# Two transformer blocks on one core: depthwise conv and its projections placed in the linear attention, layer-norm statistics in the diff heads, full-height scores, mask by VectorE

## The chip, the cores and the metric

The kernel runs on one core of a Trainium2 chip. A core has a matrix engine (TensorE, PE in the profile), three engines for elementwise work (VectorE or DVE, ScalarE or ACT, GpSimd or POOL), and SyncE (SP), which here issues all DMAs. The metric is the device time of one execution in microseconds (us). Matrix products accumulate in PSUM, which TensorE, VectorE and ScalarE reach and GpSimd does not.

## The reference, cut to what matters

Sequence 1024, width 1024, float32. A first block (grouped attention, a linear recurrence, a gated network) isn't touched. The second block computes from `h = rms_norm(x)` one wide projection, and from its parts three branches:

```python
def conv_module(a, gate, w_dw, ln_g, ln_b, w_pw):      # 31-tap causal depthwise conv, 1024 channels
    u = a * jax.nn.sigmoid(gate)
    u = lax.conv_general_dilated(u, rhs, ..., padding=[(CONV_KERNEL - 1, 0)], feature_group_count=CONV_WIDTH)
    u = jax.nn.silu(layer_norm(u, ln_g, ln_b))
    return u @ w_pw
...
# gla: 4 heads of gated linear attention, key width 128, value width 256, in chunks of 64
...
# diff_attention: 8 heads, each with two score maps of key width 64 and a value width of 128
        s = jnp.einsum('bqhtd,bkhtd->bhtqk', qi, k) * scale
        mask = key_chunk[None, :] <= q_chunk[:, None]        # chunks of 64
        p = jax.nn.softmax(jnp.where(mask, s, -jnp.inf), axis=-1)
        pd = p[:, :, 0] - lam * p[:, :, 1]
        return jnp.einsum('bhqk,bkhv->bqhv', pd, v)
...
y = (jax.nn.sigmoid(m_conv) * o_conv + jax.nn.sigmoid(m_gla) * o_gla + jax.nn.sigmoid(m_diff) * o_diff)
x = x + y @ w_out[l]
```

Then come an RMS norm and a gated feed-forward network, which aren't touched either.

## The kernel before, in words

**Data.** Activations lie with 128 channels on the partitions and 1024 positions along each, as 8 tiles of 128 x 1024. Every large product is done in three passes: both operands are split into a high part (rounded to the format fp32r) and a low part (the rest), and hi x hi, hi x lo, lo x hi are added up.

**A job** (`job`, L480) is one output tile of 128 x 1024: 8 steps over k, each with 3 passes and 2 halves of 512 columns, so 48 matmuls. Its step over one k, 6 matmuls, is called a unit here. `job(..., ks=...)` does some of the 8 units. Jobs alternate between two PSUM slots and two weight slots; a third and a fourth PSUM slot serve the attention. The jobs have a fixed order, `J_GLA`, `J_DIFF` and so on, which the host lays the weights out by. For job j SyncE loads the raw weights (`load`, L768, waits until the low part of job j-2 is made), ScalarE makes the high part (`split_act`, L455, waits until job j-2 is done), GpSimd the low part (`splits_pool`, L472). Each engine runs its own instructions strictly in the order written; semaphores order them between engines.

**Linear attention** (`gla_head_act`, `gla_head_dve`, `gla_head_pe`): 4 heads in a loop on each engine, 8 jobs each (v twice, q, k, output gate twice, mixing gate twice). VectorE makes the decayed k and q, masks the scores and adds up the states.

**Diff heads** (`diff_head_act`, `diff_head_dve`, `diff_head_pe`, L2810): head 0, heads 1 to 6 in a loop, head 7. Before head 0 stand 6 jobs. In each of heads 0 to 6 stand 6 jobs for the next head: conv gate, conv value, mixing gate, v, q, k. In head 7 stand 4 of the 8 jobs of the conv branch's mixing gate, and 4 after it. In a head the queries go in 8 blocks of 128 (qt), with (qt+1) x 128 keys each, rounded up to 256. For each block and each of the two maps t:

- TensorE: `scores2` (qt under 4: both maps in one PSUM slot) or `scores(qt, t)` (qt 4 to 7: one map at a time; t = 1 waits for the exponential of t = 0, because both use the slot). The key width is 64, so a matmul fills half of the 128 rows. The three passes of one map go to the upper rows and the others to the lower rows; for qt over 3 swapped copies let the second half of the keys use the other rows (L2846, L2847). A matmul of bf16 rows of -1e30 adds the mask (L2824).
- VectorE: the negated row maximum (L2350). ScalarE: exponential with row sum (L1796).
- VectorE, after both (`combine`): reciprocals, product with lambda, scaling of map 0 (L2358), map 1 times its factor added (L2359).
- TensorE: `turn`, transposes of the result (L2853). ScalarE: `evac`, their copy (L1801). TensorE: `pv`, product with v (L2859).

Between these, `fill(u0, u1)` lets TensorE do units of the head's jobs: 3 between the two score maps, 4 before `turn`, 1 between `turn` and `pv`, of 48 in all; head 7 takes two thirds of each count. `pv` of block 7 and the norm of a head's output (square, sum over partitions by a matmul with ones, rsqrt by Ln and Exp on ScalarE and a Newton step on VectorE) stand in the next head.

**Conv.** `taps` (L2301) are the 31 multiply-adds over 128 x 1024 on VectorE, one channel tile per diff head: the first 16 in the head before, the other 15 in the head itself, in pieces between the other VectorE work. The finished tile is added to a running sum (L2378) and stored to DRAM by SyncE.

**Tail.** After head 7: sum of the running sum (mean), 8 tiles reloaded from DRAM and centred (L2582), squared (L2013), added up (L2597), a second sum, rsqrt, then per tile scale (L2601), Silu (L2027), high part (L2031) and low part (L1630), which the 8 jobs of the conv branch's last projection (`J_PW`) need. Then come the mix of the branches, the output projection (`J_OUT2`) and the feed-forward stage.

Of the kernel before, what the change touches and what calls it, by code (L numbers as in the profile page):

```python
# [52 lines left out]
J_DIFF = J_GLA + 32  # L53
J_MC = J_DIFF + 48
J_PW = J_MC + 8
# [123 lines left out]
def two_blocks(nc, x, w, cols, consts, rope, out):  # L179
    with ExitStack() as ctx:  # L180
# [171 lines left out]
        DKL = scratch("dk_lo", [P, S], F32R, 7)
# [5 lines left out]
        CG = scratch("cg_tanh", [P, S], F32, 14)  # L358
        DO, DSQ, DV, DY = (scratch(f"do_{c}", [P, S], F32, 15 + i) for i, c in enumerate(("out", "sq", "v", "y")))
        UC = scratch("u_pad", [P, S + 32], F32, 19)  # L360
        ACC = scratch("conv_again", [P, 8, S], F32, 0)
        MC = [scratch(f"mc_tanh{i}", [P, S], F32, t) for i, t in enumerate(MC_AT)]
        LA_, LV, LYY = (scratch(f"ln_{c}", [P, S], F32, t) for t, c in ((15, "a"), (17, "v"), (18, "y")))
        SSL = scratch("ln_sum_squares", [P, S], F32, 16)
        LT = scratch("ln_mean", [P, S], F32, 11)
        SQLN = [scratch(f"ln_sq{i}", [P, S], F32, 9 + i) for i in range(2)]
        CENTRE = (2, 3, 4, 5, 6, 7, 0, 1)
        gate_spill = nc.dram_tensor("gate_spill", (P, S), F32, kind="Internal").ap()
# [411 lines left out]
        def sync_program(sp):  # L780
# [2339 lines left out]
```

## Time and profile before

| | before |
|---|---|
| time of 3 runs, us | 3457.49, 3460.99, 3462.90 |
| median, us | 3460.99 |
| profiled execution: span, us | 3460.9 |
| TensorE busy | 3361.4 us, 97% |
| VectorE busy | 2208.2 us, 64% |
| ScalarE busy | 1435.1 us, 41% |
| GpSimd busy | 1121.9 us, 32% |
| granted TensorE clock, mean | 0.990 |
| DMA, mean | 70 GB/s |

The profiled execution's own time is known by its span, from the first to the last instruction. In the profile the linear attention lies at about 1285 to 1717 us, the first 6 diff jobs at 1718 to 1784, the diff heads at 1784 to 2535, the tail after them up to about 2620. Matmuls are pipelined: the time of a single one contains its way through the array, so the distance from start to start is what counts.

### The profile page before, as it was taken

To read this page: it belongs to the slowest core of one execution; us is meant where nothing else is said; L and a number is where in the kernel's file an instruction comes from. 1 tells how busy PE (TensorE), PEld (TensorE's weight loads), DVE (VectorE), ACT (ScalarE), POOL (GpSimd) and SP (SyncE) were. 2 spreads that over 40 slices of the span, in tenths; PEclk is the share of its full clock that TensorE was granted. 3 is DMA by queue.
4 is the path that set the end of the run, shared out by engine and by line. 5 is a ranking of instruction groups with operands and counts; after the bars stand their busy time and mean duration, and the time that the engine had idled before them with its cause. 6 is when DMAs were issued, how large, how long until landed. Compare 5 with 4: busy or idle time off the path is not lost.

```text
span 3460.9 us, 44771 instructions
## 1 busy us (share of the span) xinstructions
PE 3361.4 (97%) x16616; PEld 2710.6 (78%) x16616; DVE 2208.2 (64%) x2246; ACT 1435.1 (41%) x1901; POOL 1121.9 (32%) x644
## 2 busy tenths in 40 slices
PE   8899899999999999999999999999889999999998
PEld 6677777888888868888877777777668878888886
DVE  8896968777773474322277888888856574444434
ACT  5688835444441142333223443344453353333213
POOL 2000028888832212111111111111112276766222
PEclk9999999999999999999999999999999999999999
DMA  4210221222252112111111111111122212123322
GB/s 143 62 44 19 73 88 66 84 85 79 85 196 95 47 43 92 36 42 36 36 49 43 37 42 35 38 42 36 43 79 85 79 61 91 74 90 121 134 88 83
DMA packets 59167, 242.52 MB, mean 70 GB/s; under 512 B 6592, under 2 KB 6592, under 8 KB 53312
## 3 DMA queue, kind: packets, MB, share of 16 engines
q1 hardware_dynamic: 59072, 241.22, 19.7%
q8 instruction: 63, 1.03, 0.1%
q14 instruction: 32, 0.26, 0.0%
HBM read 194.53 MB, written 41.42 MB: 68 GB/s over the span
## 4 chain that ended last, share of the span: by engine, by line
PE 81%; DVE 12%; issue 3%; ACT 3%; DMA 0%; POOL 0%; DVEq 0%; POOLq 0%; ACTq 0%
PE ps L506 45%; PE ps L1457 24%; PE ps L2696 2%; PE ps L2708 2%; PE ps L2685 1%; PE ps L2846 1%; PE ps L2859 1%; DVE conv_acc L2310 1%; PE ps L529 1%; DVE t_wide L1094 1%; PE ps L2798 1%; PE ps L2853 1%; PE ps L2832 1%; DVE small L2350 1%; PE ps L2794 1%
## 5 line engine op out<-in xcount | busy, mean ns | idle before, releaser
L477 POOL TENSOR_TENSOR w_lo_part<-w_raw,w_hi_part 128x1024 fp32r<-128x1024 f32 x162 | 404.5, 2497 | 1739.0 <-ACT w_hi_part L460 1739.0
L506 PE MATMUL ps<-h_hi_part,w_hi_part 128*128 128x512 f32 x1904 | 625.4, 409 | 34.9 <-POOL w_lo_part L477 12.4
L506 PE MATMUL ps<-h_lo_part,w_hi_part 128*128 128x512 f32 x1904 | 596.5, 394 | 0.0
L506 PE MATMUL ps<-h_hi_part,w_lo_part 128*128 128x512 f32 x1904 | 594.9, 393 | 0.0
L460 ACT ACTIVATE w_hi_part<-w_raw 128x1024 fp32r<-128x1024 f32 x180 | 189.1, 1051 | 720.0 <-PE ps L506 632.4
L506 PEld LDWEIGHTS ps<-h_hi_part,w_hi_part 128*128 128x128 f32 x1904 | 348.1, 191 | 130.4 <-issue 37.2
L506 PEld LDWEIGHTS ps<-h_lo_part,w_hi_part 128*128 128x128 f32 x1904 | 361.7, 190 | 78.5 <-issue 0.3
L506 PEld LDWEIGHTS ps<-h_hi_part,w_lo_part 128*128 128x128 f32 x1904 | 361.4, 190 | 78.7
L2310 DVE SCALAR_TENSOR_TENSOR conv_acc<-u_pad,cols,conv_acc 128x1024 f32<-128x1024 f32 x232 | 307.4, 1325 | 19.4 <-DVE conv_acc L2310 2.8
L2149 DVE TENSOR_TENSOR residual<-residual,ps 128x1024 f32<-128x1024 f32 (+1 forms) x60 | 73.2, 1221 | 268.7 <-PE ps L506 262.2
L506 PE MATMUL ps<-u_hi,w_hi_part 128*128 128x512 f32 x736 | 232.0, 390 | 0.0
L506 PE MATMUL ps<-u_lo,w_hi_part 128*128 128x512 f32 x736 | 231.2, 389 | 0.0
L506 PE MATMUL ps<-u_hi,w_lo_part 128*128 128x512 f32 x736 | 231.1, 389 | 0.0
L1457 PE MATMUL ps<-t_hi,s_hi 128*128 128x512 f32 x552 | 216.2, 392 | 1.2 <-ACT copy_x L1161 0.7
L1457 PE MATMUL ps<-t_hi,s_lo 128*128 128x512 f32 x552 | 215.2, 390 | 0.0
L1457 PE MATMUL ps<-t_lo,s_hi 128*128 128x512 f32 x552 | 214.7, 389 | 0.0
L1796 ACT ACTIVATE dprob<-ps,small 128x256 f32<-128x256 f32 (+7 forms) x128 | 94.4, 740 | 241.3 <-DVE small L2350 241.0
L506 PEld LDWEIGHTS ps<-u_lo,w_hi_part 128*128 128x128 f32 x736 | 138.2, 188 | 29.2 <-issue 0.5
L506 PEld LDWEIGHTS ps<-u_hi,w_hi_part 128*128 128x128 f32 x736 | 138.2, 188 | 29.1 <-issue 0.5
L506 PEld LDWEIGHTS ps<-u_hi,w_lo_part 128*128 128x128 f32 x736 | 138.2, 188 | 28.7
L1457 PE MATMUL ps<-b_hi,a_hi 128*128 128x512 f32 x368 | 144.0, 391 | 0.0
L1457 PE MATMUL ps<-b_hi,a_lo 128*128 128x512 f32 x368 | 143.2, 389 | 0.0
(446 smaller groups left out, 6583.1 us busy)
## 6 DMA issues: line engine op xcount, KB each, us to landing
w_raw<-in_w SPq DMA_DIRECT2D x226, 512.0 KB, 3.3
w_raw_odd<-in_w SPq DMA_DIRECT2D x46, 512.0 KB, 3.9
u_spill<-ffn_u SPq DMA_DIRECT2D x46, 512.0 KB, 3.0
u_wide<-u_spill SPq DMA_DIRECT2D x23, 1024.0 KB, 9.2
residual<-in_x SPq DMA_DIRECT2D x4, 1024.0 KB, 9.0
both_halves<-q_chan SPq DMA_DIRECT2D x16, 256.0 KB, 4.3
x_again<-in_x SPq DMA_DIRECT2D x8, 512.0 KB, 3.9
residual<-in_x SPq DMA_DIRECT2D x2, 2048.0 KB, 7.2
```

The lines of the kernel that those rows point to most:

```text
L460: act.activation(WHI[:, slot, 0:nk], WRAW[:, slot, 0:nk], ACT.Copy).then_inc(w_hi, 1)
L477: pool.tensor_tensor(WLO[:, slot], WRAW[:, slot], f32(WHI[:, slot]), ALU.subtract).then_inc(w_ready, 1)
L506: last = pe.matmul(PS[:, ps, b * HALF:(b + 1) * HALF], st[:, slot, k, :], at(mv, k, b), start=(k == 0 and n == 0), stop=(k == nk - 1 and n ...
L529: mm = pe.matmul(PS[:, slot, b * HALF:(b + 1) * HALF], ones, src[:, b * HALF:(b + 1) * HALF], start=first, stop=last)
L1094: return dve.scalar_tensor_tensor(to, a, gain, b, ALU.mult, ALU.subtract)
L1457: last = pe.matmul(bank(to), st[op][:, k, :], of[mv][:, k, :], start=(first and k == 0 and n == 0), stop=(k == 3 and n == 2), skip_group_c ...
L1796: act.activation(DP[t][:, 0:n], PS[:, 2, at:at + n], ACT.Exp, bias=small(NEGM + 2 * qt + t), accum_out=small(RSUM + 2 * qt + t)).then_inc( ...
L2149: dve.tensor_tensor(dst, src, psl(slot, True), ALU.add).then_inc(ps_free[slot], 1)
L2310: st.do(dve.scalar_tensor_tensor(ACC1[:, :], UC[:, i:i + S], wgt, ACC1[:, :], ALU.mult, ALU.add))
L2350: dve.tensor_reduce(small(NEGM + 2 * qt + t), PS[:, 2, at:at + n], AX.X, ALU.max, negate=True).then_inc(dm_ready, 1)
L2696: mm = pe.transpose(PS[:, 0, k * P:k * P + P], PR[g % 2][:, k * P:k * P + P], con("ident"))
L2708: mm = pe.matmul(PS[64 * t:64 * t + 64, 1, qt * P:qt * P + P], VT[:, k, 64 * kv:64 * kv + 64], PT[2 * (q % 2) + t][:, k, :], start=(k == 0 ...
```

## The change

The number of jobs is the same; 16 of them (conv gate and value of 8 tiles) stand in the linear attention now, two pairs per head.

- *Order of jobs.* Linear attention: v, v, q, k, conv gate, conv value, output gates, mixing gates, conv gate, conv value (12 per head). Before diff head 0: v, q, k. In diff heads 0 to 4: conv mixing gate, v, mixing gate, q, k (5 jobs, 40 units). In heads 5 and 6 the same without the conv mixing gate (32 units). In head 7: three conv mixing gates and mixing gate 7 (32 units). The last projection goes in the order 5, 6, 0, 1, 2, 3, 4, 7.
- *Loops* over heads are unrolled on all engines but GpSimd.
- *Taps.* In head h of the linear attention VectorE does all taps of tile 2h and of tile 2h-1. Tile 7 follows before and in diff head 0. Tiles are stored to DRAM as before.
- *Scores.* The moving tiles K1 (k_hi twice, one copy on each half of the rows) and K2 (k_lo and zeros), and the stationary Q1 (q_hi and q_lo), are 128 rows high: two passes per map instead of three. The number of keys is rounded less (to 128, at least 256 columns a matmul).
- *Mask.* VectorE writes -1e30 into PSUM before it takes the maximum.
- *Fills.* 21 steps in proportion to `STEPS`; `combine` scales map 0 ahead, in `scale`.
- *Statistics.* Mean in head 1; tiles reloaded, centred, squared, added up and stored again in heads 2 to 5; the variance sum in head 6; rsqrt in head 6; scale and Silu of tiles 0 and 1 in head 7.
- *Conv mixing gates* of heads 0 to 4 are stored to DRAM and reloaded in the tail.
- The norm and the add of diff head 7 stand after the second tile of the last projection.

```diff
+HEAD_JOBS = [([("mc", h)] if h < 5 else []) + [("dv", h + 1), ("md", h), ("dq", h + 1), ("dk", h + 1)] for h in range(7)]
+HEAD_JOBS.append([("mc", 5), ("mc", 6), ("mc", 7), ("md", 7)])
+PW_ORDER = (5, 6, 0, 1, 2, 3, 4, 7)
...
         def gla_head_dve(dve, st, h):
+            if h:
+                taps(dve, st, 2 * h - 1, 0, 21)
             dve.wait_ge(g_exp, h * 4 + 4)
             dve.wait_ge(job_done, 2 * jp + 3)
             dve.scalar_tensor_tensor(GB[0][:, :], psl(0), P ** -0.5, GB[0][:, :], ALU.mult, ALU.mult).then_inc(ps_free[0], 1)
+            if h:
+                taps(dve, st, 2 * h - 1, 21, 28)
...
+            if h:
+                taps(dve, st, 2 * h - 1, 28, 31)
+                conv_sum(dve, st, 2 * h - 1)
...
             states(0)
             states(1)
+            conv_u_dve(dve, n)
             states(2)
             states(3)
+            taps(dve, st, n, 0, 6)
+            gate(0)
+            taps(dve, st, n, 6, 15)
...
+            taps(dve, st, n, 15, 19)
+            gate(1)
+            taps(dve, st, n, 19, 31)
+            conv_sum(dve, st, n)
...
             def row_max(qt, t):
                 dve.wait_ge(ds_done, h * 16 + (2 * qt + t + 1))
+                st.do(dve.memset(PS[0:CH, 2, at + n - CH:at + n], -1e30))
...
+            def scale(qt):
+                dve.wait_ge(e_done, ROUNDS + h * 16 + (2 * qt + 1))
+                st.do(dve.reciprocal(small(RINV + 2 * qt), small(RSUM + 2 * qt)))
+                st.do(dve.tensor_scalar(DP[0][:, 0:n], DP[0][:, 0:n], small(RINV + 2 * qt), None, ALU.mult))
...
         def diff_k_act(act, h):
+            for t in range(2):
+                act.activation(K1[t][OWN[t], :], out_of(("dk", h), OWN[t]), ACT.Copy).then_inc(dq_hi, 1)
+            act.wait_ge(dq_hi, h * 8 + 4)
+            diff_copies_act(act, K1, K1, OTHER, OWN, LEFT)
+            split_for(act, j + 2)
...
         def diff_head_act(act, st, h):
             evac(0)
+            diff_copies_act(act, K1, K1, OTHER, OWN, RIGHT)
...
             evac(1)
+            if h < 5:
+                m_conv_act(act, h, MCS)
             exp(2, 0)
             exp(2, 1)
             evac(2)
+            if 2 <= h <= 5:
+                centred_square_act(act, 2 * h - 4)
+            if h in (5, 6):
+                diff_v_act(act, h + 1)
+            if h == 7:
+                m_conv_act(act, 5, MC[0])
             exp(3, 0)
             exp(3, 1)
             evac(3)
+            if h < 5:
+                diff_v_act(act, h + 1)
+            if h:
+                diff_rsqrt_act(act, st, h, h == 6)
+            if h == 7:
+                conv_silu_act(act, 0)
+                conv_silu_act(act, 1)
             exp(4, 0)
             exp(4, 1)
             evac(4)
...
+            diff_v_act(act, 0)
+            diff_q_act(act, 0)
+            for h in range(8):
+                diff_head_act(act, st, h)
+            act.wait_ge(job_done, J_PW)
+            conv_hi_act(act, 0)
+            diff_gate_act(act, 7)
+            conv_hi_act(act, 1)
+            for k in range(2, KT):
+                conv_silu_act(act, k)
+                conv_hi_act(act, k)
+                if k == 4:
+                    diff_sq_act(act, 8)
             diff_mean_act(act, 8)
             diff_rsqrt_act(act, st, 8)
...
+        STEPS = (2, 2, 1, 3, 1, 3, 1, 3, 1, 2, 3, 1, 2, 3, 1, 2, 3, 1, 2, 3, 1)
+        def step_at(n, units):
+            return (2 * sum(STEPS[:n]) * units + sum(STEPS)) // (2 * sum(STEPS))
...
+            def scores(qt, t):
+                n, q = max((qt + 1) * P, HALF + 256), slice(qt * P, qt * P + P)
                 if t:
+                    pe.wait_ge(e_done, ROUNDS + h * 16 + (2 * qt + 1))
+                for i, mv in enumerate((K1, K2)):
+                    pe.matmul(PS[:, 2, 0:HALF], Q1[t][:, q], mv[t][:, 0:HALF], start=(i == 0), stop=(i == 1))
+                    mm = pe.matmul(PS[:, 2, HALF:n], Q1[t][:, q], mv[t][:, HALF:n], start=(i == 0), stop=(i == 1))
+                mm.then_inc(ds_done, 1)
...
+            for ks in (range(0, 2), range(2, 4)):
                 for s in range(2):
                     job(pe, J_PW // 2, s, h_gen=GEN_LN, ks=ks)
+            job(pe, J_PW // 2, 0, h_gen=GEN_LN, ks=range(4, KT))
+            diff_sum_pe(pe, 8)
+            job(pe, J_PW // 2, 1, h_gen=GEN_LN, ks=range(4, KT))
```

## Rows read from the trace of the kernel before

**Rows 1.** The page's busy line and its chain by engine.
```profile
PE 3361.4 (97%) x16616; PEld 2710.6 (78%) x16616; DVE 2208.2 (64%) x2246; ACT 1435.1 (41%) x1901; POOL 1121.9 (32%) x644
...
PE 81%; DVE 12%; issue 3%; ACT 3%; DMA 0%; POOL 0%; DVEq 0%; POOLq 0%; ACTq 0%
```

**Rows 2.** Windows of core 0: busy us (x instructions) by engine, PEclk, DMA share, GB/s.
```profile
1501.00:1609.00 108.00, 108.00 (x551) 90.20 (x551) 30.76 (x34) 30.99 (x32) 19.38 (x8) 1.00 0.12 39
...
2071.00:2166.00 95.00, 93.55 (x497) 74.11 (x496) 79.34 (x94) 40.07 (x64) 15.74 (x7) 1.00 0.11 39
...
2451.00:2537.00 86.00, 75.94 (x383) 55.81 (x383) 53.98 (x70) 33.40 (x57) 9.73 (x4) 0.96 0.20 74
...
2482.00:2488.00 6.00, 3.44 (x13) 2.62 (x14) 5.90 (x6) 3.27 (x6) 0.00 (x0) 0.80 0.00 0
...
2537.00:2568.00 31.00, 27.79 (x118) 22.00 (x118) 27.82 (x23) 17.43 (x17) 3.14 (x2) 0.99 0.21 68
...
2568.00:2602.00 34.00, 29.86 (x100) 21.68 (x100) 19.57 (x14) 22.34 (x21) 7.85 (x3) 0.81 0.11 36
```

**Rows 3.** Chain of waits, in order of time: start us, us, what.
```profile
1576.82 11.15 PE ps L506 x48
...
1794.14 4.32 PE ps L506 x18
...
2504.60 1.39 PE ps L506 x6
...
2507.33 0.43 PE ps L2846
...
2508.27 2.96 PE ps L506 x12
```

**Rows 4.** Timeline of head 7: start us, us, engine, line, operation [idle before <-releaser].
```profile
2476.31 0.60 ACT L1801 ACTIVATE dprob_t<-ps 128x512 f32<-128x512 f32 x1 [2.45 <-PE ps L2853]
...
2478.78 1.28 ACT L1771 ACT_TABLE_LOAD   x1
...
2484.56 0.50 PE L2846 MATMUL ps<-dk_hi,dq_hi 64*128 64x512 f32 x1 [2.60 <-ACT dprob L1796]
```

**Rows 5.** Timeline of head 7, blocks with 896 keys.
```profile
2510.34 0.19 ACT L1796 ACTIVATION_READ_ACCUMULATOR dprob<-ps,small 128x1 f32 x1
...
2511.16 0.49 PE L2846 MATMUL ps<-dk_hi,dq_hi 64*128 64x512 f32 x1
...
2514.46 0.17 DVE L2356 RECIPROCAL small<-small 128x2 f32<-128x2 f32 x1 [1.17 <-ACT dprob L1796]
...
2514.86 0.69 DVE L2358 TENSOR_SCALAR dprob<-dprob,small 128x896 f32<-128x896 f32 x1
...
2516.79 0.98 PE L2853 MATMUL ps<-con,dprob 128*128 128x128 f32 x7 [0.32 <-DVE dprob L2359]
...
2518.78 1.83 PE L2859 MATMUL ps<-dprob_t,dv_tok 128*128 128x128 f32 x14 [1.01 <-ACT dprob_t L1801]
```

**Rows 6.** Timeline of the start of head 4.
```profile
2163.77 1.01 ACT L1813 ACTIVATE dv_tok<-ps 128x1024 f32<-128x1024 f32 x1
...
2165.57 1.02 ACT L1762 ACTIVATE do_sq<-ps 128x1024 f32<-128x1024 f32 x1
...
2166.06 0.39 PE L2832 MATMUL ps<-dk_hi,dq_hi 64*128 64x256 f32 x2 [0.20 <-DVE dk_lo L2365]
...
2166.65 1.98 PE L529 MATMUL ps<-do_sq,con 128*128 128x512 f32 x4
```

**Rows 7.** Groups by line and form, VectorE: count | busy us, mean ns | idle before.
```profile
L2310 DVE SCALAR_TENSOR_TENSOR conv_acc<-u_pad,cols,conv_acc 128x1024 f32<-128x1024 f32 x217 | 283.9, 1308 | 18.9 <-DVE conv_acc L2310 2.8 <-DVE conv_acc L2308 0.9
```

**Rows 8.** Groups by line (GpSimd's with min/median/max ns); TensorE's first wait of the tail.
```profile
L2027 ACT ACTIVATE conv_again<-conv_again,cols 128x1024 f32<-128x1024 f32 x8 | 9.1, 1137 | 0.0
...
L477 POOL TENSOR_TENSOR w_lo_part<-w_raw,w_hi_part x162: 2345/2404/3363, 9.6 to 3429.8; 128x1024 fp32r<-128x1024 f32 x162
...
2568.15 3.78 PE L529 MATMUL ps<-ln_sum_squares,con 128*128 128x512 f32 x4 [3.36 <-DVE ln_sum_squares L2597]
```

More of the change, by code:

```diff
@@ L52 @@
 J_GLA = J_F + 2
-J_DIFF = J_GLA + 32
-J_MC = J_DIFF + 48
-J_PW = J_MC + 8
+GLA_JOBS = 12
+J_DIFF = J_GLA + 4 * GLA_JOBS
+HEAD_JOBS = [([("mc", h)] if h < 5 else []) + [("dv", h + 1), ("md", h), ("dq", h + 1), ("dk", h + 1)] for h in range(7)]
+HEAD_JOBS.append([("mc", 5), ("mc", 6), ("mc", 7), ("md", 7)])
+DIFF_JOBS = [("dv", 0), ("dq", 0), ("dk", 0)] + [one for jobs in HEAD_JOBS for one in jobs]
+J_OF = {one: J_DIFF + n for n, one in enumerate(DIFF_JOBS)}
+J_HEAD = [J_DIFF + 3 + sum(len(jobs) for jobs in HEAD_JOBS[:h]) for h in range(9)]
+J_PW = J_DIFF + len(DIFF_JOBS)
+PW_ORDER = (5, 6, 0, 1, 2, 3, 4, 7)
 J_OUT2 = J_PW + 8
@@ L1757, in diff_sq_act, with diff_copies_act @@
+        LN_SLOT = (J_HEAD[1] + 1) % 2, (J_HEAD[6] + 1) % 2
+        def diff_copies_act(act, to, src, rows_to, rows, cols):
+            for t in range(2):
+                act.activation(to[t][rows_to[t], cols], f32(src[t][rows[t], cols]), ACT.Copy).then_inc(dq_hi, 1)
         def diff_sq_act(act, heads):
@@ L1792, in exp, with diff_head_act @@
+        def diff_head_act(act, st, h):
             def exp(qt, t):
@@ L2379, in diff_head_dve @@
[L2379 to L2386 removed]
+            if h == 0:
+                taps(dve, st, 7, 27, 29)
+            else:
+                if h < 5:
+                    dve.wait_ge(mc_out, 16 * (h + 1))
+                diff_norm_dve(dve, st, h - 1, tmp)
@@ new lines, in vector_program @@
+            taps(dve, st, 7, 0, 12)
+            diff_q_dve(dve, 0)
+            taps(dve, st, 7, 12, 18)
+            for h in range(8):
+                diff_head_dve(dve, st, h)
+            conv_scale_dve(dve, 2)
+            conv_lo_dve(dve, 0)
+            conv_scale_dve(dve, 3)
+            conv_lo_dve(dve, 1)
+            conv_scale_dve(dve, 4)
+            for k in range(2, 5):
+                conv_lo_dve(dve, k)
+                conv_scale_dve(dve, k + 3)
+            for k in range(5, KT):
+                conv_lo_dve(dve, k)
@@ L2804, in gla_head_pe @@
             sum_all(pe, 2, GB[1], True, True, con("ones")).then_inc(gsum, 1)
+            job(pe, jp + 4, 1)
+            for s in range(2):
+                job(pe, jp + 5, s)
         def diff_sum_pe(pe, heads):
@@ L2819, in fill @@
                     if ks:
[L2820 to L2833 removed]
+                        j = J_HEAD[h] + n
@@ new lines, in diff_head_pe @@
+            pe.wait_ge(vt_ready, h + 2)
+            pe.wait_ge(dq_hi, h * 8 + 6)
+            done(("dq", h))
+            done(("dk", h))
+            for qt in range(4):
+                scores2(qt)
+                if h and qt == 0:
+                    diff_sum_pe(pe, h)
+                fill(2 * qt + 1)
+                turn(qt)
+                fill(2 * qt + 2)
+                if h and qt == 0:
+                    pe.wait_ge(dmean, h + PRIMED)
+                pv(qt, h)
+                if qt == 0 and h == 1:
+                    pe.wait_ge(run_done, 1)
+                    ln_sums(LNS)
+                if qt == 0 and h == 6:
+                    pe.wait_ge(sq_used, 32)
+                    ln_sums(SSL)
```

804 lines of the change are left out of this document (419 added, 385 removed).

## The prediction, made before the changed kernel ran

> **What bounds the kernel now.** I read the page's first and fourth parts first: TensorE is busy 97% of the span and holds 81% of the chain; VectorE has 12% of it [rows 1]. The table by windows then says where TensorE isn't busy [rows 2]. A linear-attention head (108 us) has no gap, with VectorE at 30.8. A middle diff head (95 us) loses 1.45, with VectorE at 79.3. The last diff head loses 10.1, the two windows behind it 3.2 and 4.1. So TensorE bounds everything, and the change can only act on two sums: its waits from the first diff head on, 27.6 us (7 heads at 1.45, 10.1, 3.2, 4.1), and what the lowered clock takes. The granted clock is 0.96, 0.99 and 0.81 in those three windows: (0.04 x 86) + (0.01 x 31) + (0.19 x 34) = 10.2 us. Full clock is 2.4 GHz, the lower level half of it; behind the 2.60 us wait it fell to 0.80 of full in a slice of 6 us [rows 2, 4].
>
> A job (48 matmuls) takes 11.15 us alone [rows 3]. One eighth of it, a unit of 6 matmuls, is what fills the time in which scores wait for VectorE and ScalarE: 1.39 us for one unit, 2.96 for two, 4.32 for three [rows 3]. The third adds 1.36, so a job among jobs takes 10.9, wherever it stands.
>
> **Part by part.**
>
> *Jobs and taps to the linear attention.* 16 jobs move; none is added. 62 taps of 1.31 us per two tiles [rows 7] bring VectorE of a linear-attention head from 30.8 to about 30.8 + 62 x 1.31 + 5 = 117 us in 108 + 4 x 10.9 = 152 us. Before the two products that TensorE waits for stand 21 and 7 taps (27.5 and 9.2 us), beside three and one jobs (32.7 and 10.9): covered by 5 and 1.7 us, with POOL's share of the slower taps in the 1.31. Cost 0, at worst 3 heads x 3 us if a tap block runs over. SyncE's stores of the conv tiles stand between weight loads that wait longer than they do; in this stage the DMA share is 0.12 [rows 2].
>
> *Full-height scores, mask on VectorE.* The saving looks like 6 matmuls to 4, but it is not: the half-height matmuls of L2846 and L2847 run in pairs side by side. At 1024 keys six of them, 512 wide, and the mask take 0.94 us (2507.33 to 2508.27 in the chain) [rows 3]; one after the other six would take 6 x 0.227 (0.227 is 1.36 by 6) = 1.36. So four full-height ones take 4 x 0.227 = 0.91. With 640 and 768 keys (1536 columns in all) they take 0.68. What may go is the edge: two units beside a score group take 2.96, against 2 x 1.36, that is 0.24 more, and one unit between transposes and v product, all 128 rows high, only 0.03 more (1.39) [rows 3]. Per head that makes 0.2 us (edge stays) to 2.4 (edge goes, 12 groups), times 8: 2 to 19 us. I take 12, nearer to the 1.39 row. The Trainium skill (TensorEngine Tiling (Array Packing), "Key Properties") says that a change of tiling mode drains TensorE; by that rule the whole edge goes and the sum has 19 here instead of 12, a rival below. The mask becomes a memset of 64x64 in PSUM with a wait, 128 times, on VectorE's path from scores to maximum. No row has it; below it is 0 (if it were hidden), above 0.69, the scaling of 896 keys; I take 0.2, near the 0.17 of a reciprocal, the smallest VectorE row [rows 5].
>
> *The old waits go*, since the taps (41 us per head) leave VectorE: -27.6 and -10.2.
>
> *New wait 1, start of a head.* ScalarE's queue after the last job of a head is: k copy, swaps, weight split, v copy, output copy, square; TensorE's sum waits for the square and starts at 2166.65, just when it is done [rows 6]. After the change the k copy is two of 64 x 1024. ScalarE's time goes by columns (1.02 us for the 1024 of the row), so the queue is 0.95 longer. The scores themselves come no later: they need the v copy, which then ends at 2165.7, and TensorE gets to them at 2166.06 [rows 6]. Queued behind: both exponentials. With the 0.2 that is there now: 1.15 x 7, and 1.6 for head 0, which has no v product of an earlier head to cover its v copy: 9.7 us. Ends: 0 (TensorE gets there later for other reasons) and 14 (twice the new part).
>
> *New wait 2, scores(4,1).* It waits for exp(4,0), which now has in front of it on ScalarE, after evac(3): weight split and v copy (heads 1 to 4), then table, Ln, table, Exp of the normalisation. The last head of before has just this queue (with a gate in place of the v copy) and just two units to cover it: evac at 2476.31, scores(4,1) at 2484.56, 8.25 us, of which TensorE waited 2.60 [rows 4]. There evac also held TensorE up for some 0.7, since no unit stood between transposes and v product; with one there TensorE is busy for 8.25 - 2.60 - 0.7 + 1.39 - 0.4 (later start of evac, faster scores) = 5.94, so it waits 2.3, four times. Head 5 has no v copy there (8.25 - 1.95 + 0.2 = 6.5): 0.55. Head 6 has a second Ln and Exp (2.1): 2.7. Head 7 has two Silu and two table loads: 1.28 x 2 + 2.14 = 4.7 more than head 5: 5.1 (11.1 against 5.94). Sum 9.2 + 0.55 + 2.7 + 5.1 = 17.5 us. Ends: 9 (head 7 and 6 only, plus 1.2) and 24. The skill (ScalarE: Activation LUTs, "What ACT_TABLE_LOAD costs") gives a switch of tables 1283 ns and a drain of some 1380 more. In the trace the first load starts at 2478.78 and scores(4,1) at 2484.56; two loads, Ln, Exp and exp(4,0) are 2 x 1.28 + 2 x 1.06 + 0.99 = 5.67 of these 5.78, so there is no room for a drain [rows 4], and it is left out; with it head 7 would wait 2.8 longer.
>
> *New wait 3, thinner fills.* Before, 48 units over 21 steps; now 40 in heads 0 to 4 and 32 in heads 5 to 7, as head 7 had. What must be covered, read in the last head for 896 keys [rows 5]: from the scores' start to the next scores 3.3 us (2507.26 to 2510.6; two units reach to 2511.16), from scores to transposes 5.63 (2511.16 to 2516.79). The split of `combine` takes the scaling (0.72) off this path, the mask puts 0.2 on it: 5.15, and 5.6 for 1024 keys, 4.65 for 768, 4.3 for 640. With 40 units the steps round to 2 (qt 4), 3, 3, 3 units: cover 3.8, 5.1, 5.3, 5.4; missing 0.5 + 0 + 0 + 0.3 = 0.8 us per head, 5 heads: 4. With 32 units they round to 2, 2, 3, 2, one of the first steps to 1 and one step before pv to 0: missing 0.2 and 0.6 (qt 2, 3), 0.5, 0.9, 1.1 (1 unit under 3.6), 1.0 (evac unhidden, as the 1.01 of [rows 5]), 1.7: 6.0 per head, 3 heads: 18. Together 22 us; ends 10 and 32.
>
> *Statistics in the heads, tail.* Centring, squares and sums (8 x 1.2 on each engine) stand in heads 2 to 5 where VectorE is idle by half: 0. Behind the last job TensorE does v product, 16 units and one sum, 25.5 us. The tiles come from ScalarE: copy k0 1.1, diff gate 2.0, copy k1 1.1, table 1.3, six times Silu and copy (1.14 + 1.06, 2.25 with the hand-over) [rows 8], the last head's two reads 2.05, VectorE's low part 1.2: the last at 22.2. TensorE then has one unit, the sum and four units to do (1.4 + 2.0 + 5.5), until 31.0: 5 us of waits in all. Then ScalarE waits for the last head's sum, runs mean, Ln, Exp with two tables (5.9) and only then splits the weights of the third projection job: 25.6 + 5.9 + 1.0 + POOL's 2.4 [rows 8] = 34.9, TensorE being free at 31.0: 3.9. Together 8.9; ends 4 and 14. Queued behind that weight split is every later one. Old tail waits are in the 27.6. SyncE: four reloads of tiles stand behind a weight load that waits for the split at 4.7; they land at 9, in time for k = 7. Extra DMAs (10 of gates, 16 more of tiles) ride in a DMA share of 0.11 [rows 2].
>
> *Clock.* Behind a wait of 3.36 us the four sum matmuls took 3.78 us [rows 8] instead of 1.98 [rows 6], and the window has 0.81 [rows 2]; the 2.60 cost 0.20 x 6 = 1.2 in its slice [rows 2] and some behind it. I price waits over 2 us: 4 x 1.5 (heads 1 to 4), 1.5 (head 6), 2.4 (head 7), 6.3 (tail, as before) = 16.2. Ends: 6 and 26.
>
> *Sum:* 3460.9 - 12 - 27.6 - 10.2 + 9.7 + 17.5 + 22 + 8.9 + 16.2 = 3485.4. The profiled span is 3460.9 and the median of three runs 3460.99, so nothing is added for what lies around the span.
>
> **Rivals.**
> A, faster: ScalarE's queue and the units are no limit, because row maxima come early once the taps are gone. The slots that decide are scores(4,1) of heads 1 to 4 and the steps of heads 5 to 7: if their waits stay under 1 us per head and only head 7, the head starts and the tail pay (1.15 x 7 + 5.1 + 8.9 + clock 8 = 30), the time is 3460.9 - 49.8 + 30 = 3441. For it: VectorE falls from 79 to about 45 of 85 us. Against: the 2.60 row, which wasn't VectorE's doing. It turns from gain to loss once waits and clock exceed 49.8 us.
> B, nearly even: the edge of the scores goes whole (19 rather than 12) and the small waits don't pull the clock down (16.2 becomes 8): 3470. This is the page's drain rule's case.
> C, worse: the wait of 1.15 at each head start lowers the clock too (7 x 1.5 = 10.5), the thin fills of heads 5 to 7 do (3 x 2), and taps run over in the linear attention (9): 3511. For it: nothing but the taps' 1.7 us of slack. Against: a middle head waits 1.45 at full clock [rows 2].
>
> **Chances.** Forecast 0.47 (own range 3474 to 3500), A 0.2, B 0.15, C 0.18. The range goes from A to C with half of each outside: 3438 to 3514. This kernel's measurement can't tell 0.2% (7 us) from nothing. A falls under that; B holds most of the middle (0.11); slower is the forecast, C and the rest of B: 0.7.
>
> **What would show it.** Heads 1 to 4 about 87 us apart, with TensorE waiting for dprob of L1796's counterpart 2.3 us once per head; a wait for the square at each head's start; heads 5 to 7 with 8 to 12 us of waits each; linear-attention heads of 152 us without a gap; score groups of 0.91 at 1024 keys; one wait of 4 us for POOL's split behind the last diff head. If TensorE's waits there sum to under 45 us, or the linear-attention heads show gaps, the forecast is wrong.

## The result, and the profile after

The changed kernel takes 3492.9 us (median of 4 runs, 3491.1 to 3495.5), the kernel before 3461.9 beside it: ratio 1.0093, 95% interval [1.0081, 1.0105]. It is slower by 31 us, 0.9%; 3485 was forecast. The profiled execution spans 3490.7 us, 29.8 more than that of before, and the forecast's sum was for this figure: +24.5. The stages ahead of the linear attention, the same in both kernels, happen to take 3.5 us less in the profiled execution of the changed one (1283.2 against 1286.7), and the stages from 2781.0 before and 2810.7 after to the end take 680 us in both. Between these two points, where the change acts, 33.2 us are added (before, then after, columns as in [rows 2]):

```profile
1286.70:2781.00 1494.30, 1465.08 (x7361) 1181.41 (x7360) 941.18 (x1017) 553.21 (x752) 270.14 (x111) 0.99 0.15 51
...
1283.20:2810.70 1527.50, 1458.12 (x7042) 1194.66 (x7040) 996.93 (x1191) 566.81 (x765) 270.01 (x111) 0.99 0.18 58
```

TensorE's busy time falls by 7.0 us there, and the time in which it isn't busy rises by 40.2, from 29.2 to 69.4.

The page's first and fourth parts, after:

```profile
PE 3351.6 (96%) x16296; PEld 2721.3 (78%) x16296; DVE 2261.3 (65%) x2420; ACT 1448.7 (42%) x1914; POOL 1124.3 (32%) x644
PE 78%; DVE 13%; ACT 5%; issue 2%; DMA 0%; POOL 0%; POOLq 0%; DVEq 0%; ACTq 0%; SPq 0%
```

TensorE has lost a point of its share, and ScalarE now holds 5% of the chain [rows 1 for before]. Where, the table by windows tells: linear-attention head 1, diff heads 0, 2, 5, 6 and 7, and the stretch behind the last head (columns as in [rows 2]):

```profile
1402.40:1560.10 157.70, 154.18 (x743) 128.63 (x742) 125.05 (x100) 35.61 (x38) 31.13 (x13) 0.98 0.15 47
...
1946.00:2028.30 82.30, 79.79 (x405) 65.68 (x403) 51.15 (x94) 35.58 (x60) 12.61 (x6) 0.98 0.14 45
...
2115.70:2201.40 85.70, 81.67 (x409) 66.71 (x409) 45.90 (x87) 42.98 (x67) 11.95 (x5) 0.98 0.17 56
...
2372.70:2451.70 79.00, 70.67 (x361) 56.20 (x361) 45.38 (x86) 41.21 (x65) 9.58 (x4) 1.00 0.18 54
2451.70:2534.50 82.80, 72.45 (x365) 56.99 (x365) 44.03 (x85) 42.12 (x66) 9.55 (x4) 1.00 0.11 32
2534.50:2598.20 63.70, 53.81 (x261) 42.66 (x261) 32.48 (x67) 30.38 (x51) 5.72 (x2) 0.97 0.12 42
2598.20:2660.00 61.80, 52.14 (x221) 40.82 (x222) 39.10 (x34) 34.74 (x35) 10.37 (x4) 0.92 0.32 111
```

Length less TensorE's busy time: 3.5 us in a linear-attention head (three such heads, 10.6 in all), where [rows 2] had none; 4.0 in each of diff heads 1 to 4; 8.3, 10.4, 9.9 and 9.7 in the last four rows. VectorE is at 46 of 86 us in a middle diff head, so it did stop being busy there; the waits are larger all the same.

What TensorE waited for between 1280 and 2700 us (total, times, longest):

```profile
PE ps L3049 <- ACT dprob L1910: 21.1, 10, 5.4
PE ps L3056 <- DVE dprob L2547: 16.2, 20, 1.8
PE ps L2947 <- DVE gla L2370: 10.6, 3, 3.5
PE ps L537 <- ACT do_sq L1856: 7.6, 7, 1.1
PE ps L514 <- DVE h_lo_part L2524: 4.0, 3, 2.8
PE ps L514 <- POOL w_lo_part L485: 3.8, 1, 3.8
PE ps L3062 <- ACT dprob_t L1915: 3.0, 3, 1.0
PE ps L3040 <- ACT dv_tok L1921: 2.0, 1, 2.0
```

L3049 are scores that wait for the exponential, L3056 transposes that wait for the combined tile, L3062 the v product, L537 the sum that waits for the square, L2947 the transposes of a linear-attention head that wait for its second product.

The chain of waits through diff head 3, as in [rows 3, 4] (start, us, what):

```profile
2229.69 1.28 ACT L1865
2230.99 1.06 ACT do_y L1865
2232.07 1.28 ACT L1868
2233.36 1.06 ACT do_y L1868
2234.42 0.78 ACT dprob L1910 x2
2235.24 0.50 PE ps L3049
2236.26 4.31 PE ps L514 x12
...
2244.31 2.75 PE ps L514 x12
2247.75 4.14 PE ps L514 x18
```

Table, Ln, table, Exp and the exponential stand in a row, and scores(4,1) come at 2235.24 after a wait of 2.35 us. The same two units take 4.31 us right behind that wait and 2.75 a few steps on: 1.56 us of clock, in each of heads 1 to 4. The granted clock of a window of 3 us behind the wait is 0.51; behind the wait of 1.09 us at the head's start it is 1.00:

```profile
2236.00:2239.00 3.00, 3.00 (x9) 2.37 (x8) 1.53 (x5) 0.88 (x2) 0.00 (x0) 0.51 0.01 5
2202.00:2205.00 3.00, 3.00 (x12) 1.98 (x11) 0.86 (x4) 1.14 (x2) 0.00 (x0) 1.00 0.89 279
```

Two and three units without a wait take 2.75 and 4.1, where [rows 3] had 2.96 and 4.32.

In linear-attention head 1 (timeline; PE rows of the jobs left out):

```profile
1478.03 7.24 DVE L2443 SCALAR_TENSOR_TENSOR conv_acc<-u_pad,cols,conv_acc 128x1024 f32<-128x1024 f32 x4
1481.58 2.61 POOL L485 TENSOR_TENSOR w_lo_part<-w_raw,w_hi_part 128x1024 fp32r<-128x1024 f32 x1 [9.75 <-ACT w_hi_part L468]
...
1481.99 3.28 DVE L2443 SCALAR_TENSOR_TENSOR conv_acc<-u_pad,cols,conv_acc 128x1024 f32<-128x1024 f32 x1
...
1485.31 1.22 DVE L2370 TENSOR_TENSOR gla<-ps,gla 128x1024 f32<-128x1024 f32 x1
...
1486.59 0.69 PE L2947 MATMUL ps<-con,gla 128*128 128x128 f32 x2 [3.52 <-DVE gla L2370]
```

Four taps take 7.24 us; at the median of 1.285 they would take 5.14. Three of them do take 1.28 us; the fourth, which starts at 1481.99 while GpSimd splits a weight, takes 3.28, 2.0 more, and ends 1.08 us after the split does (1484.19). The other three taps of these 28 that start during a split take 3.30 to 3.32 us and also end 1.08 us after it.

### The profile page after: what moved, and what is told of

Same layout as the page of the kernel before. It is cut to its first block, busy times and chain, and to the rows that moved or that the text cites. A ratio compares the mean times of both kernels' runs of the same rounds, so it can differ in the third digit from the quotient of the medians.

```text
span 3490.7 us, 42900 instructions
## 1 busy us (share of the span) xinstructions
PE 3351.6 (96%) x16296; PEld 2721.3 (78%) x16296; DVE 2261.3 (65%) x2420; ACT 1448.7 (42%) x1914; POOL 1124.3 (32%) x644
## 4 chain that ended last, share of the span: by engine, by line
PE 78%; DVE 13%; ACT 5%; issue 2%; DMA 0%; POOL 0%; POOLq 0%; DVEq 0%; ACTq 0%; SPq 0%
PE ps L514 42%; PE ps L1523 24%; DVE conv_acc L2443 4%; PE ps L2907 2%; PE ps L2895 2%; PE ps L2884 1%; PE ps L3062 1%; PE ps L3056 1%; PE ps L3049 1%; DVE t_wide L1160 1%; PE ps L537 1%; DVE small L2533 1%; PE ps L2997 1%; DVE dprob L2547 1%; ACT w_hi_part L468 1%
## 5 line engine op out<-in xcount | busy, mean ns | idle before, releaser
L514 PE MATMUL ps<-h_hi_part,w_hi_part 128*128 128x512 f32 x1904 | 617.3, 405 | 37.8 <-POOL w_lo_part L485 16.2
L2443 DVE SCALAR_TENSOR_TENSOR conv_acc<-u_pad,cols,conv_acc 128x1024 f32<-128x1024 f32 x232 | 334.8, 1443 | 7.4
L2532 DVE MEMSET ps<- 64x64 f32 x128 | 14.3, 112 | 206.4 <-PE ps L3041 103.5
```

The source lines that it names most:

```text
L514: last = pe.matmul(PS[:, ps, b * HALF:(b + 1) * HALF], st[:, slot, k, :], at(mv, k, b), start=(k == 0 and n == 0), stop=(k == nk - 1 and n ...
L2443: st.do(dve.scalar_tensor_tensor(acc[:, :], UC[:, i:i + S], wgt, acc[:, :], ALU.mult, ALU.add))
```

## Experiments

Each is the changed kernel with one edit, run five times beside 8 or 9 runs of the kernel before, whose medians were 3458.9 to 3460.9. Differences below are from 3492.9, the changed kernel's median. They carry the scatter of stages that no edit touches: up to the first sum of the linear attention the traces of these kernels have 1400.2 to 1405.7 us. So the length of the stage an edit acts in is given too, between matmuls that every one of these traces has: the linear attention from its first to its fourth sum (473.3 us in the changed kernel), the diff heads from there to the last matmul of the eighth sum of squares (763.8), the tail from there to the last matmul of the sum of squares in the RMS norm that follows (173.1).

The theory was: the forecast is near for the wrong reason. The scores give back some 10 us more than I had booked, and the taps, booked at nothing, take it away again. The rival: the booked terms hold, and the taps' waits only stand in for others.

**Taps shared out anew.**

```
-                taps(dve, st, 2 * h - 1, 0, 21)
+                taps(dve, st, 2 * h - 1, 0, 18)
-                taps(dve, st, 2 * h - 1, 21, 28)
+                taps(dve, st, 2 * h - 1, 18, 23)
-                taps(dve, st, 2 * h - 1, 28, 31)
+                taps(dve, st, 2 * h - 1, 23, 31)
```

> The changed kernel with the odd tile's taps in linear-attention heads 1 to 3 shared out as 18, 5 and 8 around the two products and the mask copy, in place of 21, 7 and 3; nothing else. Theory (tap blocks run over): TensorE's wait of 3.5 us for the second product in each of three heads and the lowered clock behind it are both the doing of those five extra taps; the heads fall from 157.3 to about 152.5 us each, the whole from 3492.9 to about 3478 (10.6 us of waits and some 3 to 6 of clock gone). Rival (the taps only expose it): VectorE's work in these heads is held up by GpSimd's weight splits, so the time lost moves to the states or to the gates behind them; a wait of over 1 us shows up there and the whole stays within 3 us of 3492.9.

Measured: 3472.8 us, ratio 1.0043 [1.0029, 1.0057]: 20.2 less than the changed kernel. The table by windows for head 1:

```profile
1400.00:1552.50 152.50, 152.50 (x746) 126.79 (x745) 126.27 (x101) 36.19 (x38) 31.48 (x12) 1.00 0.15 49
```

TensorE has no gap, at full clock. From the sum in head 0 to that in head 3 it is 455.8 us in the trace (1400.2 to 1856.0), where the changed kernel has 473.3 (1400.5 to 1873.8): 17.5 less, 10.6 of them waits and the rest nearly all clock behind them. Another 2.3 us lie behind that stretch, 1.4 of them in the diff heads, where the granted clock fell less often though the waits of 2.35 us are all there. In head 3 of this run scores(4,1) start at 2215.97 behind 2.35 us, and the clock stays up:

```profile
2216.00:2219.00 3.00, 3.00 (x14) 2.53 (x15) 1.60 (x4) 0.89 (x2) 0.00 (x0) 1.00 0.19 75
```

So the 1.56 us behind such a wait are what four heads of the changed kernel paid, not a fixed price; what decides between the two isn't shown.

**GpSimd's weight splits shortened.** It leaves out seven eighths of the weights' low part in the 48 jobs of the linear attention (the last argument: 1 of 8 blocks of 128 columns).

```
-            splits_pool(pool, J_FFN + 2, J_FFN2)
+            splits_pool(pool, J_FFN + 2, J_GLA)
+            splits_pool(pool, J_GLA, J_DIFF, 1)
+            splits_pool(pool, J_DIFF, J_FFN2)
```

> The changed kernel in which GpSimd computes only the first eighth (128 columns) of the low part of each weight for the 48 jobs of the linear attention; it leaves out the rest of that low part. Taps stay shared out 21, 7 and 3. Theory (taps run over because VectorE's operations last 3.3 us instead of 1.3 where they meet a weight split on GpSimd, four times in the 28 taps): the taps' mean falls from 1443 ns to about 1290, the 28 taps and what stands with them take 8 us less, the three waits of 3.5 us and the slow clock behind them go, heads of 157.3 come to about 152.7: 3492.9 to about 3478, as with the taps shared out anew. Rival (28 taps are too many whatever GpSimd does): the waits stay above 2 us and the time above 3487.

Measured: 3474.2 us, ratio 1.0040 [1.0026, 1.0054]; no wait for the second product is left, with 21, 7 and 3 taps unchanged, and the same stretch has 455.8 us again. The taps, by lines (busy us, mean ns), here and before them on the page of the changed kernel:

```profile
L2446 DVE SCALAR_TENSOR_TENSOR conv_acc<-u_pad,cols,conv_acc 128x1024 f32<-128x1024 f32 x232 | 303.2, 1307 | 7.4
```

```profile
L2443 DVE SCALAR_TENSOR_TENSOR conv_acc<-u_pad,cols,conv_acc 128x1024 f32<-128x1024 f32 x232 | 334.8, 1443 | 7.4
```

The mean falls by 136 ns. That settles the cause: it isn't 28 taps that are too many, but 28 taps of which four meet a weight split. Instructions of 128 x 1024 on VectorE with one input in PSUM didn't pay in the changed kernel: an add at 1391.95 took its usual 1.22 us inside a split of 2.41.

**Half-height low part.**

```
-                for i, mv in enumerate((K1, K2)):
-                    pe.matmul(PS[:, 2, 0:HALF], Q1[t][:, q], mv[t][:, 0:HALF], ...)
+                for i, (mv, r) in enumerate(((K1, slice(0, P)), (K2, OWN[t]))):
+                    pe.matmul(PS[:, 2, 0:HALF], Q1[t][r, q], mv[t][r, 0:HALF], ...)
...
```

The narrow blocks (qt under 4) are cut the same way, with both full-height matmuls ahead of the two half-height ones.

> The changed kernel with the second matmul of each score pair (low part of k) cut back to the 64 rows that hold data, so each score group goes from full height to half height and back; the same columns, the same number of instructions. Theory (the edge is what full height took away): 12 groups a head cost about 0.2 us more each; heads 0 to 4 grow by 2.0 to 2.4 us each, heads 5 to 7 by less, since part of it lies in waits; the whole goes to about 3508 (3503 to 3512). Rival (no edge; the gain on scores was fewer matmuls and the mask that left TensorE): nothing changes, 3492.9 within 3.

Measured: 3516.5 us, ratio 1.0167 [1.0153, 1.0181]: 23.5 more, above the 3512 that I had as upper end, and 23.5 more in the diff heads alone (787.3). Its chain in head 3, three and two units beside the scores:

```profile
2259.72 4.31 PE ps L514 x18
...
2281.55 2.96 PE ps L514 x12
```

These are 4.14 and 2.75 in the changed kernel and 4.32 and 2.96 in [rows 3]: about 0.2 us comes back behind a group as soon as half of its matmuls are 64 rows high. Columns and instructions are the same. The expectation stopped there, but the group itself gets longer too: in the chain at 1024 keys 1.13 us (2280.42 to 2281.55) instead of 0.93 (2353.41 to 2354.34 in the changed kernel, one head on), since it now changes height in its middle. A head of 85.7 us has 88.4, 2.7 more; that is a net figure, with 0.7 us less of waits in it (scores(4,1) wait 1.9 instead of 2.35). So this run shows that a change of height costs, and isn't a measure of what the scores of before cost, which had no change inside a group.

**The v copy behind exp(4,1).**

```
             evac(3)
-            if h < 5:
-                diff_v_act(act, h + 1)
...
             exp(4, 1)
+            if h < 5:
+                diff_v_act(act, h + 1)
             evac(4)
```

> The changed kernel with ScalarE's weight split and copy for the next head's v moved, in heads 0 to 4, from behind the transposes' eviction for the fourth query tile to behind the second exponential of the fifth; nothing else. Theory (ScalarE's queue sets scores(4,1)): 1.95 us less stand before exp(4,0), so the wait of 2.3 us in heads 1 to 4 falls to about 0.3 and the slow clock behind it (12 matmuls in 4.3 us rather than 2.75) goes: heads of 85.7 us come to about 82.5, the whole from 3492.9 to about 3478 to 3481. Rival (row maxima or the rest of the queue set it): the wait only moves to the transposes' eviction for the fifth query tile, since the copy now stands before it: heads keep 85 us or more and the whole moves by under 4 us.

Measured: 3490.1 us, ratio 1.0089 [1.0075, 1.0102]: 2.9 less, and 3.8 less in the diff heads (760.0). The wait at scores(4,1) did fall to 0.48 us. But (timeline of the same head):

```profile
2241.07 2.54 POOL L485 TENSOR_TENSOR w_lo_part<-w_raw,w_hi_part 128x1024 fp32r<-128x1024 f32 x1 [20.92 <-ACT w_hi_part L468]
2241.27 3.41 DVE L558 TENSOR_TENSOR do_newton<-do_y 128x1024 f32<-128x1024 f32 x1
...
2249.46 0.50 PE L3049 MATMUL ps<-dk_hi_twice,dq_hi_lo 128*128 128x512 f32 x1 [1.35 <-ACT dprob L1910]
```

GpSimd's split moved along with the copy and met VectorE's first correction step, 3.41 us instead of the 1.22 it had before. The maximum of the next tile stands behind it, and scores(5,1) waited 1.35. The rival had the size (under 4 us), at another place; neither foresaw that the split moves along. The queue was rightly named, and most of the gain was given back one tile later.

**One table for Ln and Exp, loaded early.**

```
             exp(3, 1)
+            if h:
+                tables(act, LOG_AND_EXP)
             evac(3)
```

> The changed kernel with the table that holds both Ln and Exp loaded in heads 1 to 7 while ScalarE waits for the transposes of the fourth query tile, so that the load before Ln is taken off the queue in front of exp(4,0) and the load before Exp moves to the gate's Tanh; nothing else. Theory (ScalarE's queue between that eviction and exp(4,0) sets scores(4,1), and the v copy was the wrong part to move because GpSimd's weight split went with it onto VectorE's correction steps): 2.56 us less stand in front, the wait of 2.35 us in heads 1 to 4 goes to 0 with the slow clock behind it, head 6 loses about 2.5 of wait, head 7 about 1.3 (its second Silu load stays): 3492.9 to about 3474 (3470 to 3478). Rival (anything taken off that queue comes back at the next slot, as when the v copy was moved): the transposes or scores of the next tile wait instead and the whole stays above 3488.

Measured: 3472.6 us, ratio 1.0039 [1.0025, 1.0052]: 20.3 less, 19.7 in the diff heads (744.1). Timeline in head 3, and TensorE's waits for the exponential:

```profile
2217.88 1.28 ACT L545 ACT_TABLE_LOAD   x1
...
2222.68 1.06 ACT L1865 ACTIVATE do_y<-do_v 128x1024 f32<-128x1024 f32 x1
...
2223.77 1.06 ACT L1868 ACTIVATE do_y<-do_y 128x1024 f32<-128x1024 f32 x1
...
2224.74 0.78 ACT L1910 ACTIVATE dprob<-ps,small 128x640 f32<-128x640 f32 x1
```

```profile
PE ps L3051 <- ACT dprob L1910: 6.0, 4, 2.7
```

The load lies in ScalarE's idle time, Ln, Exp and the exponential follow each other, and 21.1 us of waits in ten places are 6.0 in four. Heads 2 to 5 start 82.3 us apart instead of 85.7. That is 2.35 of wait and 1.56 of clock, less 0.6 that the transposes of the same tile now wait for VectorE. Over all heads such waits for the combined tile rise from 16.2 to 19.4. So ScalarE's queue between that eviction and exp(4,0) was the bound of new wait 2, and 3.2 of the 15.1 us came back as other waits.

**The sum behind two units.**

```
-                if h and qt == 0:
-                    diff_sum_pe(pe, h)
                 fill(2 * qt + 1)
+                if h and qt == 0:
+                    diff_sum_pe(pe, h)
```

> The changed kernel with the sum over the squares issued on TensorE behind the two units that follow the first scores of a head, in place of ahead of them; nothing else. Theory: the square is then ready, the wait of 1.1 us at each of seven head starts goes, and nothing else waits longer since mean and transposes are covered: 3492.9 to about 3485. Rival: the sum's later end delays the mean on ScalarE and with it the eviction and the v product of the first query tile; under 3 us in all.

Measured: 3481.5 us, ratio 1.0059 [1.0045, 1.0072]: 11.4 less. The seven waits for the square (7.6 us) are gone. The four sum matmuls count 1.72 us in the chain instead of the 1.98 behind a wait; 0.16 of that is only their way through the array, which the chain counts behind a wait alone (from first start to last end the timeline has 1.88 and 1.98). The diff heads are 8.3 us shorter (755.5). The other 3 us lie in stages that the edit doesn't touch.

**The third projection job's weight split ahead of the mean.**

```
+            split_act(act, J_PW // 2 + 1, 0)
             diff_mean_act(act, 8)
```

> The changed kernel with ScalarE's weight split for the third projection job put ahead of its read of the last head's sum instead of behind Ln and Exp; nothing else. Theory: TensorE's wait of 3.8 us for GpSimd's low part of that weight goes, with about 1 us of clock: 3492.9 to about 3488. Rival: the mean, Ln and Exp come 1 us later and the y of the last head, or the two jobs before, wait for it instead; within 1 us of no change.

Measured: 3487.1 us, ratio 1.0080 [1.0067, 1.0094]: 5.8 less, and 6.4 less in the tail (166.7). The wait of 3.8 us is gone, and none took its place there.

**The two Silu behind the last head.**

```
-            if h == 7:
-                conv_silu_act(act, 0)
-                conv_silu_act(act, 1)
...
             act.wait_ge(job_done, J_PW)
+            conv_silu_act(act, 0)
             conv_hi_act(act, 0)
-            diff_gate_act(act, 7)
+            conv_silu_act(act, 1)
             conv_hi_act(act, 1)
+            diff_gate_act(act, 7)
```

> The changed kernel with the first two Silu of the convolution tiles taken out of the last head and put behind it, ahead of their copies; nothing else. Theory: in the last head 4.8 us (two loads at 1.28, two Silu at 1.15) leave the queue in front of exp(4,0), so its wait of 5.4 us falls to about 0.6 and the slow clock behind it goes (-6); behind the head one load and two Silu (3.6 us) stand in front of TensorE's first unit and come back as waits there: net -1 to -3, 3490 to 3492. Rival: the tail's queue has room while TensorE does the first v product, and the whole gain of 6 stays: 3487.

Measured: 3491.7 us, ratio 1.0084 [1.0070, 1.0098]: 1.2 less, which this comparison can't tell from nothing.

```profile
PE ps L3048 <- ACT dprob L1910: 16.2, 10, 2.5
...
PE ps L514 <- DVE h_lo_part L2523: 7.3, 2, 4.4
```

These were 21.1 and 4.0 in the changed kernel: of 4.9 us saved in the head, 3.3 are waited for in the tail. Diff heads and tail have 764.1 and 172.4 us, against 763.8 and 173.1. The 5.1 booked for head 7 was real, but not to be had by this move.

**Units of the thin heads shared out otherwise.**

```
+        THIN = (2, 1, 1, 2, 1, 2, 1, 2, 0, 2, 2, 1, 2, 2, 1, 2, 2, 1, 2, 2, 1)
         def step_at(n, units):
+            if units == 32:
+                return sum(THIN[:n])
```

> The changed kernel with the 32 units of heads 5 to 7 shared out by hand (2, 2, 1 for each of the four wide query tiles, one unit less behind the fourth tile), so that no step of the seventh tile has 1, 3, 0; nothing else. Theory (in thin heads only the sum of the units counts, what a step lacks another has over): the wait for the seventh tile's eviction (1.0) and for scores(6,1) (1.1) go in three heads, half of it comes back elsewhere: 3492.9 to about 3490. Rival: each step's cover is its own and the old waits go whole: 3486.

Measured: 3492.2 us (3487.0 to 3499.2), ratio 1.0088 [1.0074, 1.0101]: no difference that these runs can tell. The profiled execution is the slowest of the five.

```profile
PE ps L3060 <- DVE dprob L2547: 19.4, 22, 1.8
PE ps L3053 <- ACT dprob L1910: 19.0, 7, 5.8
...
PE ps L3066 <- ACT dprob_t L1915: 2.1, 3, 0.7
```

40.5 us in all, against 21.1 + 16.2 + 3.0 = 40.3. In a head with too few units it is their number that counts; a step that gets one more has it from another that then waits. That stands against my reading that each step rounds for itself.

**Four edits together** (taps, weight split in the tail, tables, sum).

> The changed kernel with four single edits at once: taps shared out 18, 5, 8; the third projection job's weight split ahead of the mean; the table with Ln and Exp loaded during the fourth tile's transposes; the sum over squares behind two units. Theory (the four losses are independent, so the times measured one by one add: -20.2, -5.8, -20.3, -11.4): 3492.9 - 57.7 = 3435, range 3431 to 3442, and so 0.7% under the kernel before. Rival (queue slots share their slack): the earlier sum or loads take back part of each other's room, 3445 to 3455.

Measured: 3441.3 us (3440.6 to 3443.1), ratio 0.9946 [0.9933, 0.9960]: faster than the kernel before by 0.54% and than the changed one by 1.5%. 51.6 us less than 3492.9, where the four single differences make 57.7. By stages nothing is missing: the single edits took 17.5 from the linear attention, 19.7 and 8.3 from the diff heads and 6.4 from the tail, 51.9 in all, and together they take 17.6, 27.9 and 6.4, 51.9 again. The four are independent, and the 6 us are scatter in the medians. TensorE's waits from 1280 to 2700 us:

```profile
PE ps L3060 <- DVE dprob L2551: 18.6, 24, 1.8
PE ps L3053 <- ACT dprob L1910: 6.0, 4, 2.7
PE ps L514 <- DVE h_lo_part L2528: 3.5, 2, 2.8
PE ps L3066 <- ACT dprob_t L1915: 3.0, 3, 1.0
PE ps L3044 <- ACT dv_tok L1921: 2.0, 1, 2.0
```

What is left is new wait 3, 2.7 us at scores(4,1) of the last head and a part of the tail.

**The same with the two Silu moved.**

> The four edits and the first two Silu of the convolution tiles moved behind the last head. Theory: by itself that move brought 1.2 us because the tail took back what the head gained; with the tail's weight split already early the tail has no more room than before, so 3434, within 2 us of the kernel with four edits. Rival: with the tables of Ln and Exp in one load the last head had still 2.7 us of wait in front of scores(4,1), which now goes with its slow clock, while the tail hides the Silu: 3430.

Measured: 3443.6 us, ratio 0.9952 [0.9939, 0.9966]: no gain here either. TensorE's waits for the exponential fall from 6.0 to 3.3 us, and those for the low part in the tail rise from 3.5 to 7.1.

## Why the prediction was right in sign and near in size

*Waits.* From diff head 0 to the third projection job they were forecast at 58.1 us and are 58.7 by the windows (56.7 from 1946.0 on, and 2.0 ahead of it, for the v copy of head 0). By kind, from the table of waits:

| term | forecast | measured |
|---|---|---|
| new wait 1: square 7.6, v copy of head 0 2.0 | 9.7 | 9.6 |
| new wait 2: scores(4,1), 4 x 2.35 + 0.5 + 2.5 + 5.4 | 17.5 | 17.8 |
| new wait 3: 16.2 + 3.0, and the other scores' 21.1 - 17.8 | 22 | 22.5 |
| tail: 4.0 + 3.8 | 8.9 | 7.8 |

These were read from the last head of before, which already ran with thin fills and the full queue [rows 4, 5]. The old waits came to 28.8 us, not 27.6: the seventh of the heads booked at 1.45 lost 2.65. For the waits 2 and 1 the runs show the mechanism as well (tables, late sum). Wait 3 has the right sum, but the rounding of single steps isn't its mechanism.

*Scores: the term that was too small.* -12 was forecast, with -19 if the whole edge goes. Between the two points of the table at the start, TensorE's busy time falls by 7.0 us, though it works at the lower clock for 44.4 us instead of 20.5. While busy that costs it 20.2 us instead of 9.4, half of the busy time at that level. Without the clock the matmuls are thus 17.7 us shorter, and the jobs among them are the same; what is left are the score groups, with the mask and the lesser rounding of keys in it. The chain shows the edge itself: two units behind a group take 2.75 instead of 2.96, three take 4.14 instead of 4.32. About 0.2 for 96 groups is 19. Why I erred: one row of 1.39 for full-height neighbours was there, and I took less than the whole edge all the same. What the Trainium skill (TensorEngine Tiling (Array Packing), "Key Properties") says of a change of tiling mode, that it drains TensorE, fits the trace: 2.96 against 2.75 for the same two units.

*Taps: the step that failed.* "Cost 0, at worst 3 heads x 3 us if a tap block runs over." It ran over in all three heads: 10.6 us of waits and 6.1 of clock while busy, 17.5 in the trace, of which 0.8 is not placed (20.2 and 18.8 in the medians of the two runs). By the forecast's own sign, linear-attention heads of 152 us without a gap, this part was wrong: they have 157 to 158 us and 3.5 of wait each. The 1.31 us per tap was a mean over diff heads, where few taps met a weight split; in the linear attention four of the 28 started during one, at some 2.0 us more each. 28 x 1.31 = 36.7 was booked; the two blocks take 0.74 + 32.45 + 11.19 = 44.4. The subtraction ahead of them met a split too (3.35 instead of 1.22). 7.7 + 2.1 = 9.8 us too much, against 5 + 1.7 of slack, leaves 3.1; the wait is 3.5. Rival C had this overrun, but at 9 us and with no cause beside the slack.

*Clock.* 16.2 was forecast from diff head 0 on; by the granted clock it is 14.1 us of TensorE's busy time from the fourth sum of the linear attention to 2810.7. The places differ: head 0, booked at nothing, has a lowered clock behind its wait of 2.0 us, and head 6, booked at 1.5, has 1.00 throughout. The 1.5 behind a wait over 2 us is 1.56 in the chain, but not always there (taps run above). Rival C's idea that 1.15 us lowers the clock too doesn't hold: it is 1.00 behind the 1.09 of head 3. Nor do the thin fills of heads 5 and 6, 1.00 in both rows of the table.

*The sum again.* Where the change acts, 33.2 us were added, against 24.5:

| | forecast | measured |
|---|---|---|
| TensorE not busy | -27.6 + 58.1 = +30.5 | +40.2 |
| lowered clock | -10.2 + 16.2 = +6.0 | 20.2 - 9.4 = +10.8 |
| matmuls without the clock | -12 | -17.7 |

The taps are in the first line with 10.6 and in the second with 6.1: 16.7 us in no term. Against them stand -5.7 at the matmuls, -0.9 at the other waits, old and new, and -1.3 at the other clock.

*Rivals.* A (faster, 3441) fell: scores(4,1) of heads 1 to 4 waited 2.35 us each with VectorE half idle. B had the scores nearly right and missed the taps; B's scores and C's taps together are what happened. That the time fell within 8 us of the forecast is luck in part: errors of 16.7 and -7.9 us cancelled by half, and in the profiled execution untouched stages gave back 3.5 more.

## What to carry to other kernels

When work moves to a stage where another engine is busy, take its duration from rows that meet that engine's work, not from a mean elsewhere, and compare the excess with the slack. To tell whether edits add up, compare the stages that they act in, not only medians of the whole. A queue of one engine in front of a fixed slot can be priced well from the one place in the trace that already has that queue. Before moving an item off such a queue, list what moves with it on other engines; a table load that slid into idle time gave little back (3.2 of 15.1 us).

## What the runs showed of the hardware

- In the stages of this change, a VectorE instruction of 128x1024 with both inputs in SBUF that starts while GpSimd splits a weight of 128x1024 ends some 1.08 us after the split's end, so it takes up to 3.3 or 3.4 us instead of 1.22 to 1.29: taps (up to 3.32), a correction step (3.41), and the scaling of a convolution tile in the tail (3.41 at 2614.19, GpSimd's split from 2614.04 on) alike. A split that starts during a tap takes longer itself (3.44 instead of 2.40 at 1447.16, where the tap beside it kept its 1.28). With one input in PSUM VectorE took 1.22 as ever (at 1391.95, inside a split of 2.41).
- Full-height work behind half-height matmuls takes 0.18 to 0.21 us longer (4.32 against 4.14, 2.96 against 2.75); a group that goes from full to half height in its middle is 0.20 longer besides (1.13 against 0.93 at 1024 keys).
- The same wait of 2.35 us in the same place left TensorE at a granted clock of 0.51 in one kernel and 1.00 in another (head 3, changed kernel and taps run).
- One load of the table that holds Ln and Exp (1.28 us) serves both and the softmax's exponential behind them; in head 3 the next load came at 2244.13, before Tanh, where ScalarE had 0.75 us to spare after it, and TensorE did not wait.
